# Prompt attention: the turn of the weights three steps behind the scores instead of two, value products and result copies one step later

## The reference, cut to what matters

```python
def fox_attend(q, c_q, pos_q, k, v, c_k, pos_k):
    s = jnp.einsum('bqhd,bkhd->bhqk', q, k).astype(jnp.float32) * (HEAD_DIM_B ** -0.5)
    bias = c_q (queries) - c_k (keys)          # cumulated log forget gates
    s = jnp.where(pos_k <= pos_q, s + bias, -jnp.inf)
    p = jax.nn.softmax(s, axis=-1)
    return jnp.einsum('bhqk,bkhd->bqhd', p.astype(v.dtype), v)
```

## Time and profile before

| | before |
|---|---|
| median of 3 runs | 2788.17 us |
| the profiled execution | 2791.05 us |
| its span, first to last instruction | 2789.4 us |
| PE, DVE, ACT, POOL busy | 92%, 51%, 26%, 17% of the span |
| chain that ended last, by engine | PE 79%, POOL 9%, DVE 6%, ACT 3% |
| granted TensorE clock, mean | 0.961 |

### The profile page before, as it was taken

One profiled execution on the slowest core, in us unless ns is written; L12 is line 12 of the kernel. 1 busy time (PEld: TensorE's weight loads), 2 busy tenths in 40 slices (PEclk: granted clock), 3 DMA queues, 4 the chain that ended last, 5 costly groups with the idle time before them and its releaser, 6 DMA issues.

```text
span 2789.4 us, 36789 instructions
## 1 busy us (share of the span) xinstructions
PE 2578.4 (92%) x15741; PEld 2497.2 (90%) x15741; DVE 1414.1 (51%) x1957; ACT 735.8 (26%) x1202; POOL 481.1 (17%) x436
## 2 busy tenths in 40 slices
PE   5987958887999999999999899999999999999995
PEld 5987846666999999999999789989999999999994
DVE  2689966655763333333335754467433333333356
ACT  3100046654441111111112532134211111111133
POOL 2289963320310000000001310023000000000022
PEclk7998979998999999999999999999999999999998
DMA  7211040055211111111112321142111111111121
GB/s 212 48 33 30 15 150 9 9 147 161 76 46 45 39 43 42 46 46 46 46 46 81 108 82 46 45 130 61 46 46 46 46 46 45 34 43 46 46 91 65
DMA packets 217922, 173.38 MB, mean 62 GB/s; under 512 B 9121, under 2 KB 195601, under 8 KB 217752
## 3 DMA queue, kind: packets, MB, share of 16 engines
q1 hardware_dynamic: 211488, 159.41, 19.2%
q0 software_dynamic: 4960, 11.49, 1.3%
q10 hardware_dynamic: 1320, 0.24, 0.1%
HBM read 152.45 MB, written 18.93 MB: 61 GB/s over the span
## 4 chain that ended last, share of the span: by engine, by line
PE 79%; POOL 9%; DVE 6%; ACT 3%; issue 2%; DMA 1%; SPq 0%; DVEq 0%; ACTq 0%; POOLq 0%
PE PS L663 24%; PE PS L664 24%; PE PS L665 24%; POOL S L551 4%; POOL HF L552 3%; PE PS L835 2%; DVE ST L1580 1%; ACT PB L1130 1%; DMA RAW<-in_w_in_even 1%; DVE WLO L1425 1%; DVE RSD L1704 1%; PE PS L677 1%; PE PS L798 1%; PE PS L678 1%; PE PS L815 1%
## 5 line engine op out<-in xcount | busy, mean ns | idle before, releaser
L663 PE MATMUL PS<-AH,WHI 128*128 128x368 f32 x3360 | 1128.4, 336 | 61.5 <-DVE QKV L1539 28.7
L664 PE MATMUL PS<-AL,WHI 128*128 128x368 f32 x3360 | 1122.1, 334 | 0.0
L665 PE MATMUL PS<-AH,WLO 128*128 128x368 f32 x3360 | 1117.4, 333 | 0.0
L663 PEld LDWEIGHTS PS<-AH,WHI 128*128 128x128 f32 x3360 | 641.3, 191 | 69.8 <-DVE QKV L1539 32.2
L664 PEld LDWEIGHTS PS<-AL,WHI 128*128 128x128 f32 x3360 | 640.5, 191 | 2.5 <-issue 0.4
L665 PEld LDWEIGHTS PS<-AH,WLO 128*128 128x128 f32 x3360 | 640.6, 191 | 0.0
L1769 DVE TENSOR_TENSOR HF<-S,PS 128x368 f32<-128x368 f32 x132 | 71.0, 538 | 678.7 <-ACT S L1068 678.7
L663 PE MATMUL PS<-HH,WHI 128*128 128x368 f32 x1056 | 353.6, 335 | 24.6 <-issue 16.7
L1053 ACT CAST WHI<-RAW 128x1024 fp32r<-128x1024 f32 x224 | 223.6, 1047 | 538.4 <-PE PS L665 531.2
L664 PE MATMUL PS<-HL,WHI 128*128 128x368 f32 x1056 | 352.9, 334 | 0.0
L665 PE MATMUL PS<-HH,WLO 128*128 128x368 f32 x1056 | 352.3, 334 | 0.0
(11 more groups left out here) (265 smaller groups left out, 1942.0 us busy)
## 6 DMA issues: line engine op xcount, KB each, us to landing
RAW<-in_w_ffn_gate SPq DMA_DIRECT2D x52, 512.0 KB, 3.9
RAW<-in_w_ffn_up SPq DMA_DIRECT2D x52, 512.0 KB, 4.9
RAW<-in_w_ffn_down SPq DMA_DIRECT2D x52, 512.0 KB, 3.5
RAW<-in_w_in_even SPq DMA_DIRECT2D x20, 512.0 KB, 4.9
Y<-x_spill SPq DMA_DIRECT2D x12, 736.0 KB, 8.1
RAW<-in_w_out_even SPq DMA_DIRECT2D x16, 512.0 KB, 4.8
RAW<-in_w_in_odd SPq DMA_DIRECT2D x16, 512.0 KB, 4.1
RAW<-in_w_out_odd SPq DMA_DIRECT2D x16, 512.0 KB, 4.8
```

The lines of the kernel that those rows point to most:

```text
L663: pe.matmul(out, wh, xh, start=first, stop=False)
L664: pe.matmul(out, wh, xl, start=False, stop=False)
L665: return pe.matmul(out, wl, xh, start=False, stop=last)
```

## The change

The turn and its copies move from unit n-2 to unit n-3 in the loops of PE, ACT and DVE; V moves from even n to odd n, one step later; the result copies move from odd n to even n, one step later, and the loops are one step longer. POOL's and SP's lists are as before.

```diff
 # PE
-            for n in range(NU + 4):
+            for n in range(NU + 5):
                 if n < NU:
                     scores(*ATT[n])
-                if 2 <= n < NU + 2:
-                    turn(*ATT[n - 2])
-                if n >= 4 and n % 2 == 0:
-                    values(ATT[n - 4], ATT[n - 3])
+                if 3 <= n < NU + 3:
+                    turn(*ATT[n - 3])
+                if n >= 5 and n % 2 == 1:
+                    values(ATT[n - 5], ATT[n - 4])
 # ACT
-            for n in range(NU + 5):
+            for n in range(NU + 6):
                 if n < NU:
                     expo(*ATT[n])
-                if 2 <= n < NU + 2:
-                    turned(*ATT[n - 2])
-                if n >= 5 and n % 2 == 1:
+                if 3 <= n < NU + 3:
+                    turned(*ATT[n - 3])
+                if n >= 6 and n % 2 == 0:
+                    result(*ATT[n - 6])
                     result(*ATT[n - 5])
-                    result(*ATT[n - 4])
 # DVE
-            for n in range(NU + 2):
+            for n in range(NU + 3):
                 if 1 <= n < NU + 1:
                     inverse(*ATT[n - 1])
                 if n < NU:
                     peak(*ATT[n])
-                if n >= 2:
-                    turned(*ATT[n - 2])
+                if n >= 3:
+                    turned(*ATT[n - 3])
```

## The result

| | before | after |
|---|---|---|
| median | 2788.45 us (6 runs) | 2800.18 us (6 runs, 2797.63 to 2801.21) |
| ratio, 95% interval | | 1.0043 (1.003 to 1.0056) |
| span of the profiled execution | 2789.4 us | 2798.1 us |
| first score to the last V of the prompt attention | 186.46 us | 197.70 us |

The account below looks back on a forecast made before the run. The prediction took prompt attention to be bound by a circle of hand-overs (V, scores, maximum, exponential, result copies). 2.5 us at the start, 3 cycles x 1.1 and 0 at the end made +5.9: median 2794.1 us, range 2785 to 2801.

Parts of the forecast that it names:

- the circle of the earlier trace: Prompt attention: V, scores, maximum, exponential, result copies, V; seven of nine V start 0.14 or 0.15 us behind result copies.
- POOL's wait, 0 us: PE's weight loads for the turn wait 11.0 us for POOL; DVE's copy comes last, so 0 us is recovered.
- gone by name: Sign in the changed profile: the turn's wait for POOL gone by name, the wait for DVE's copies still there.
- Parity, +1.1 us a cycle: Result copies follow exponentials of even, not odd n; nine V-to-V intervals sum to 46.75 us after, 45.63 before.
- The nine carriers: Units whose lead, maximum and exponential carry the circle: odd r1 to r17 before (22.1 us), even r0 to r16 after (24.1).
- Start and end: Ends of the prompt attention: V(r4,r5) first comes 2.5 us later; the end takes 28.9 us on both sides, 0.
- I take no more drops than before: PE's granted clock in prompt attention: no added drops; bounds -3 us with none left, +8 with a long one every cycle.
- rival 4: Circle plus a long clock drop in every cycle, adding 3 to 8 us: 2797 to 2802 us; chance 0.18.
- The forecast's own 2790 to 2798: Span of the main case, parity counts and the clock falls as before: 2794 us, chance 0.46.
- the stretch that the prediction had named: Thin 16-row units, V(r6,r7) and V(r8,r9): 11.5 us against 10.2, longer and emptier, which favours more clock drops.
- Rival 2: PE's wait for POOL was real in 12 places: 11.0 us go, 2777 us; chance 0.12.
- rival 3: No difference: odd and even carriers even out because more V hang on DVE's total work; 2788 to 2791 us, chance 0.24.

Follow-up runs that it names:

- experiment 3: Kernel before, with ACT copying the results of a pair ahead of the exponential of odd n instead of behind it: 2783.83 us, 0.9984 of before.
- experiment 4: Kernel after, with ACT copying the results of a pair ahead of the exponential of even n instead of behind it: 2794.15 us, 1.0018 of before.
- experiment 10: Kernel before with the turn at n-3, V one step later still at even n, and result copies ahead of the exponential of odd n: 2775.99 us, 0.9956.
- experiment 5: Kernel before without POOL's multiply of the weights; the turn waits for the exponential instead: 2789.49 us, 1.0001 of before.
- experiment 6: Kernel after plus 13 unused score products a cycle in the turns of r6, r8 and r10 (the filled after): 2790.51 us, 1.0001 of before.
- experiment 7: Kernel before plus six unused score products a cycle in the turns of r8 and r10 (the filled before): 2785.57 us, 0.9991 of before.
- experiment 1: Kernel after, with V one step later at even n and result copies one step later at odd n; turn stays at n-3: 2781.26 us, 0.9977 of before.
- experiment 2: Kernel before, with V one step later at odd n and result copies one step later at even n; turn stays at n-2: 2792.43 us, 1.0015 of before.
- experiment 8: Kernel after, with V issued ahead of the turn in its step on PE: 2826.84 us, 1.014 of before.
- experiment 9: Kernel before, with V issued ahead of the turn in its step on PE: 2817.93 us, 1.0101 of before.
- experiment 12: Kernel after, with turns and copies of the two 1040-column units r8 and r10 alone one step earlier: 2806.8 us, 1.006 of before.
- experiment 11: Kernel before, with turns and copies of the two 1040-column units r8 and r10 alone one step later: 2788.37 us, 0.9999 of before.

## Why the side was right and the size was not

**What bounds the stage.** Right, with a limit. Moving the result copies by a few places in ACT's list moves the time (experiments 3, 4, 10), so the circle of the earlier trace rows binds. But the prediction did not see how near the second path is: in before, an open circle is worth 1.0 us a cycle, though seven V of nine hang on it by the rows. The second V of the earlier trace rows, at 481.82, shows the other path itself. Between the result copies and V stands the second part of a turn, which waited for ACT's copy:

```profile
481.16 0.55 PE L815 MATMUL PS<-CST,PB 128*128 128x128 f32 x3 [0.18 <-ACT PT L1137]
```

It ends at 481.71, 0.04 us after the result copies. With these out of the way, in experiment 3, the interval to this V is 5.64 us instead of 5.81.

**POOL's wait, 0 us.** Right: without the multiply the time stays (experiment 5, 1.0001). The Trainium skill ("Perfetto Trace Analysis", Optimization Strategy, not the section that the prediction names) says that consistent bubbles can mean too little room for the next tile. No run here adds a buffer, so that is not shown. One sign was wrong, though: the wait was to be gone by name. The waits of after still have it:

```profile
PE PS L815 <- DVE PT L1590: 19.2, 28, 1.3
...
PEld PS L815 <- POOL PB L572: 12.6, 10, 1.6
```

12.6 us in 10 places, although the multiply that a turn needs now ended a step earlier. In time order of after:

```profile
499.96 0.91 POOL L572 TENSOR_SCALAR PB<-PB,ST 128x768 f32<-128x768 f32 x1 [1.99 <-DVE ST L1584]
...
500.77 0.68 DVE L1590 COPY PT<-PS 128x512 f32<-128x512 f32 x1
...
501.57 0.53 PEld L815 LDWEIGHTS PS<-CST,PB 128*128 128x128 f32 x5 [1.55 <-POOL PB L572]
```

The turn at 501.57 is that of r4, 640 columns wide, whose own multiply had ended at 497.98; the multiply at 499.96 has 768 columns and is another unit's. The name follows what ended nearby, and the turn starts 0.12 us behind DVE's copy as in the earlier trace rows.

**Parity, +1.1 us a cycle.** Right as a sum: 46.75 worked out, 46.60 in experiment 6 at full clock, against 45.67 in experiment 7, so +0.9. The nine carriers by their stated steps add up to some 22.3 and 24.3, not 22.1 and 24.1; the difference of 2.0 stands. The intervals, in us (before at full clock, the last two columns the second cycle of each trace; three forecasts, for (r10,r11), (r12,r13) and (r16,r17), are given without their working):

| V | before | forecast | after, filled | after |
|---|---|---|---|---|
| (r6,r7) | 5.56 | 6.4 | 6.19 | 6.19 |
| (r8,r9) | 4.62 | 5.1 | 5.13 | 6.46 |
| (r10,r11) | 4.09 | 4.6 | 4.53 | 5.18 |
| (r12,r13) | 5.39 | 5.4 | 5.43 | 5.43 |
| (r14,r15) | 5.81 | 3.8 | 3.96 | 3.95 |
| (r16,r17) | 4.32 | 4.6 | 4.68 | 4.68 |
| (r0,r1) | 4.99 | 5.4 | 5.40 | 5.41 |
| (r2,r3) | 4.60 | 5.8 | 5.64 | 5.64 |
| (r4,r5) | 6.23 | 5.7 | 5.64 | 5.64 |

No interval of the filled kernel is off by more than 0.21 us. Unfilled, two stand out, V(r8,r9) and V(r10,r11), by 1.33 and 0.65 us: the ones that lie in the stretches at 0.87 and 0.67.

That the +0.9 is parity's alone, as the prediction has it, is not so. The edit changes parity and depth at once, and the cycles at full clock are 45.63 us before, 44.37 in experiment 1, 46.60 in experiment 6 and some 46.3 in experiment 2. By these parity costs 2.2 us a cycle with the deep turn and some 0.7 with the shallow one, and the depth, for which the prediction has no term of its own, gains 1.3 with V at even n and costs some 0.3 with V at odd n. The intervals came out because they were worked through the new lists, where both changes stand.

**Start and end.** From the first score to V(r4,r5) it was 17.70 us and is 19.99: +2.29 for the 2.5. From the last V(r4,r5) to the last V it is 28.98 in the filled kernel before and 28.87 in the filled one after, for the 28.9 on both sides; unfilled, 30.52 after. At full clock the whole stage grows by 188.61 - 183.71 = 4.9 us for the 5.9 of the sum.

**The clock: the step that failed.** "I take no more drops than before" was the choice, with bounds of -3 and +8. Drops cost before 186.46 - 183.71 = 2.75 us and after 197.70 - 188.61 = 9.09: +6.3, within the bounds and not at the value taken. 4.9 + 6.3 = 11.2 is the 11.24 that the stage grew by. That the added products did no more than hold the clock is borne out by the first cycle of after: its V(r8,r9) comes before the fall and takes 5.11 us, where the filled kernel takes 5.13, and the other rows of the table agree. So what happened is rival 4, the forecast's own sum and the clock on top of it, with 2797 to 2802 us for the 2800.18 measured. The forecast's own 2790 to 2798 was missed; the stated range holds the result because it was drawn to take in most of rival 4. The clock falls in every cycle, in or right behind the stretch that the prediction had named: the interval to V(r6,r7) is at 1.00 in all four, the one to V(r8,r9) is drawn out in three, the one to V(r10,r11) in all. The prediction had the evidence that pointed there, a stretch of 11.5 us for 10.2 with the same PE work in it, and chose by the number of cycles that fell before (one in four), which says little about a longer stretch. The Trainium skill ("TensorE: Matmul & The Clock Gate", What's actually happening) has the engine's recent activity set the gate; experiments 6 and 7 agree, since there only activity was added and the clock stayed at 1.00. Experiment 2 fits too: the clock falls in each of its cycles, and a V of 30 products takes up to 3.41 us in them.

**Rival 2** (POOL) fell with experiment 5, **rival 3** (no difference) with the filled kernels: even at full clock the cycle differs by 0.9 us and the stage by 4.9.

**What stays open.** Why the deep turn with V at even n gains 1.26 us a cycle over before, and why opening the circle there gives 1.54 more (44.37 to 42.83) when it gives 1.0 in before. Why the deeper turn gains nothing when V stands at odd n. Experiments 8, 9 and 12 put other waits in place of the ones they removed, and 11 explains a part.

## What to carry to other kernels

Where a copy that frees a bank stands in an engine's fixed order behind another unit's work, ask which unit that is: here, with the turn three steps behind, it decided between some -7 and +12 us against before, about half of it through the clock, and moving the copy ahead of that work won some 5 to 6 us in each of three kernels. When a change thins out a stretch of TensorE's work, price the clock for that stretch by what the same instructions take at the lower level, and count it in the likeliest case if the stretch gets longer. Before believing the engine that a wait names, look at which of its semaphores came last in time order.

## What the runs showed of the hardware

Products that compute nothing made the kernel after 9.7 us faster: of 13 a cycle, each of 512 columns, 9 lie in the thin stretch and 4 just ahead of it, and the stretch went from 12.65 us at a granted clock of 0.87 to 11.32 at 1.00. PE made no long pause before it lost its clock: in the cycle of after shown above these are its longest idle times from r6's turn to the V at 465.81, which took 2.82 us.

```profile
458.28 0.63 PE L815 MATMUL PS<-CST,PB 128*128 128x128 f32 x4 [1.11 <-DVE PT L1590]
...
464.25 0.39 PE L815 MATMUL PS<-CST,PB 16*128 16x16 f32 x4 [0.71 <-DVE PT L1590]
...
465.28 0.44 PE L815 MATMUL PS<-CST,PB 16*128 16x16 f32 x5 [0.63 <-ACT PT L1137]
```

The 5.18 us behind the thin stretch, in which PE is busy throughout by the records, still ran at 0.67.
